# Reordering VectorE's work in the attention half of a two-layer hybrid encoder: rotary in two parts at other steps, low weight halves ahead of the attention step, two last output units interleaved

## The chip, the cores and the metric

The kernel runs on one core of one Trainium2 chip. A core has TensorE (PE, matrix multiply), VectorE (DVE), ScalarE (ACT), GpSimd (POOL) and SyncE (SP, which here only issues DMAs). The metric is the device time of one execution in microseconds, and lower is better. Times are medians of several executions.

## The reference, cut to what matters

```python
for l in range(2):
    u = rmsnorm(h, norm_g[l])
    p = u @ w_in[l]                      # 528 tokens x 1024, times 1024 x 9216
    hq, hf_f, hf_b, hi, hgt, aq, ak, av, agt = split(p)
    o_h = hgrn2_mixer(hq, hf_f, hf_b, hi, hgt, ...)      # 8 heads, gated linear recurrence
    o_a = diff_attention_mixer(aq, ak, av, agt, ...)     # 8 heads: rotary on q and k, two
                                         # softmaxes per head, p0 - lam * p1, times v, norm, gate
    h = h + concat(o_h, o_a) @ w_out[l]  # 2048 x 1024
return rmsnorm(h, final_norm_g)[:, 16:]
```

Rotary turns each pair of rows of q and k: `t1*c - t2*s, t2*c + t1*s`. Everything is float32.

## The kernel before, in words

Activations lie transposed: 128 rows of features on the partitions, 528 tokens (16 meta tokens and 512 real ones) along the free axis. All matrix work with weights is cut into **units**: one unit is 1024 x 128 weights, 8 **pieces** of 128 x 128. A layer has 89 units. To keep float32 accuracy with a rounded format, weights and activations are each split in a high and a low half, and a piece is three products (high-high, high-low, low-high), each in two matmuls of 264 tokens, so 6 matmuls; in layer 1, where only real tokens matter, units of q, gates and outputs take one matmul of 512 in place of two. Line 1256 is the matmul of every piece.

Each unit passes through a chain. SP loads `w_raw` (2 buffers) once `lo_cut` says that the raw buffer has been used; ACT copies it to `w_hi` (line 556, `cut_high`, 3 buffers), right after it evacuated the unit three places before; DVE subtracts to make `w_lo` (line 889, `cut_low`); PE runs the unit's 8 pieces into one of two PSUM buffers `proj`, and its first piece waits for `lo_cut` and for the buffer to have been evacuated. What follows a unit on DVE is `follow`: for `aq` and `ak` the rotary, which is a swap of neighbouring rows (line 983), two multiplications (lines 985 and 986) and an addition (line 991) into `gate_f`; for `outA` and `outB`, the units of the output projection, an addition onto `h` (line 943).

There is no planner at run time. Every engine executes a list written by the same loops: 16 heads per layer (0 to 7 HGRN2, 8 to 15 attention), and 13 **steps** per head. In each step an engine does its part of the head (`hgrn` or `attend`) and then its part of the units that feed the next head. PE spreads the next head's pieces over the steps by tables of shares (`HG_FEED`, `AT_FEED`, and `LAST_FEED` for head 15, where the fed units are `outB0` to `outB3`, with 7 pieces each, since the eighth needs head 15's own output). `units_after(c, s)` says which units PE has finished by the step before, so that ACT evacuates them at step s; `units_followed` says when DVE follows them, `units_cut` when DVE makes the low half of the unit three places on.

An attention head has 5 blocks of queries in layer 0 and 4 in layer 1 (128 queries, or the 16 meta tokens), each with two components, one per step. In a step PE makes the scores (4 matmuls, lines 1420 and 1422) in the one PSUM buffer `pair`; DVE takes the row maximum (line 1162, `neg_max`); ACT exponentiates (line 731, `decay`) and so frees `pair` for the next step's scores. In even steps from 2 on DVE combines the two softmaxes of the block before (lines 1181, 1183, 1191, `qk_dec`), PE transposes the result in the odd step after (lines 1449, 1450), ACT copies it out (lines 762, 765, `cols`), and PE multiplies it by v (lines 1435, 1437) one step later. DVE's order within a step before the change is: its part of the head, then `stack_low` if it is due, then `follow`, then the low half of a unit (`cut_after`).

Before head c's first scores, `gate_f` is split again: ACT makes the high halves in `q_stack` and `k_stack` (`stack_high`, line 774, after step 9 of the head before, after step 11 of head 7), DVE makes the low halves (`stack_low`, line 999, one step later), and SP copies them across partitions by DMA. In an attention head, the output of the head before is scaled, transposed and gated in steps 1 and 2 (lines 1101, 1117, `mixed_t`), rounded by ACT in step 3 (line 784, `mix_hi`) and its low half made by POOL (line 529, `mix_lo`). In head 15, the last piece of each `outB` unit (k = 6) needs this of head 14.

Of the kernel before, what the change touches and what calls it, by code (L numbers as in the profile page):

```python
# [38 lines left out]
HG_HEADS = 8  # L39
# [67 lines left out]
HG_FEED = (2, 3, 3, 3, 3, 3, 4, 4, 3, 3, 3, 4, 2)  # L107
AT_FEED = (3, 3, 3, 2, 2, 3, 2, 3, 2, 3, 2, 2, 2)

LAST_FEED = (2, 2, 1, 1, 3, 3, 3, 3, 2, 3, 2, 2, 1)  # L110

# [30 lines left out]
def pieces_per_unit(c):  # L144
    return EARLY_K if c == HEADS - 1 else KT


def pieces_by(c, s):

    if s < 0:  # L150
        return 0
    first, last = fed_units(c)
    pieces = (last - first) * pieces_per_unit(c)
    return round(share_fed(c, s) * pieces)


def units_after(c, s):

    first, _ = fed_units(c)
    n = pieces_per_unit(c)  # L160
    return range(first + pieces_by(c, s - 2) // n, first + pieces_by(c, s - 1) // n)


def unit_of(tile):
# [37 lines left out]
def units_followed(c, s):  # L202

    if c == HG_HEADS - 1:

        first = fed_units(c)[0]
        units = {TURN_KEYS: [first], TURN_KEYS + 1: [first + 1, first + 2]}.get(s, [])  # L210
    elif not HG_HEADS < c < HEADS - 1:
        units = [*units_after(c, s)]
    elif s % 2 == 1:
        units = [*units_after(c, s - 2), *units_after(c, s - 1)]
    else:
        units = []
    if s == 1 and c > 0:
        units = [*units_not_followed(c - 1), *units]
    return units


def units_not_followed(c):
# [6 lines left out]
def encoder_trunk(nc, x_t, w_units, norm_g, lb_logits, hg_gain, lambdas, at_gain, final_g,  # L229
# [12 lines left out]
    with ctx:  # L242
# [589 lines left out]
        def _(dve):  # L832
# [7 lines left out]
            def after(w):  # L840
                dve.wait_ge(dve_step, w)

            def prepare_lower_bounds():

                dve.wait_ge(consts_in, 16 * 8)
                w = step(dve.tensor_tensor(lb_work[:, 2, :], lb[:, 0, :], lb[:, 1, :], ALU.max))
                after(w)
                step(dve.tensor_tensor(lb_work[:, 0, :], lb[:, 0, :], lb_work[:, 2, :], ALU.subtract))
                dve.tensor_tensor(lb_work[:, 1, :], lb[:, 1, :], lb_work[:, 2, :], ALU.subtract)\
                    .then_inc(lb_max, 1)  # L850
                w = step(dve.tensor_tensor(lam_prod[:, :, :], lam_in[:, :, 0, :], lam_in[:, :, 1, :],
                                           ALU.mult))
                after(w)
                dve.tensor_reduce(lam_sum[:, :, :].rearrange("p a b -> p (a b)"), lam_prod[:, :, :],
                                  axis=X, op=ALU.add).then_inc(lb_max, 1)
                dve.wait_ge(lb_exp, 1)
                w = step(dve.tensor_tensor(lb_work[:, 2, :], lb_work[:, 0, :], lb_work[:, 1, :], ALU.add))
                after(w)
                w = step(dve.reciprocal(lb_work[:, 3, :], lb_work[:, 2, :]))
                after(w)  # L860
                step(dve.tensor_tensor(lb_work[:, 0, :], lb_work[:, 0, :], lb_work[:, 3, :], ALU.mult))
                w = step(dve.tensor_tensor(lb_work[:, 1, :], lb_work[:, 1, :], lb_work[:, 3, :], ALU.mult))
                after(w)
                w = step(dve.tensor_tensor(lb_work[:, 2, :], lb_work[:, 0, :], lb_work[:, 1, :], ALU.add))
                after(w)
                step(dve.tensor_tensor(lb[:, 0, :], lb_work[:, 0, :], lb_work[:, 0, :], ALU.subtract))
                w = step(dve.tensor_tensor(lb[:, 1, :], lb_work[:, 2, :], lb_work[:, 0, :], ALU.subtract))
                after(w)
                dve.tensor_scalar(one_minus_lb[:, :, :], lb[:, :, :], -1.0, 1.0, ALU.mult, ALU.add)\
                    .then_inc(bounds_ready, 1)  # L870
                dve.wait_ge(bounds_ready, 1)
                dve.wait_ge(lb_exp, 2)
                for l in range(DEPTH):
                    init = 0.8 - 0.6 * math.exp(-0.3 * l)
                    w = step(dve.tensor_tensor(lam[:, l:l + 1], lam_sum[:, l, 0:1], lam_sum[:, l, 1:2],
                                               ALU.subtract))
                    after(w)
                    step(dve.tensor_scalar(lam[:, l:l + 1], lam[:, l:l + 1], -1.0, -init, ALU.mult, ALU.add))

                    step(dve.tensor_scalar(g_at[:, l:l + 1], g_at[:, l:l + 1],  # L880
                                           math.sqrt(P) * (1.0 - init) * 0.5, None, ALU.mult))
                step(dve.tensor_scalar(g_hg[:, :], g_hg[:, :], math.sqrt(P), None, ALU.mult))
                w = step(dve.tensor_scalar(g_final[:, :], g_final[:, :], math.sqrt(D_MODEL), None, ALU.mult))
                after(w)
# [50 lines left out]
            def follow(l, i):  # L935
# [39 lines left out]
                elif what == "g":  # L975
                    dve.tensor_tensor(gates[:, c % 2, ts], a, b, ALU.mult).then_inc(stage_read, 1)
                elif what == "ag":
                    dve.scalar_tensor_tensor(gates[:, c % 2, ts], a, 1.0, b, ALU.add, ALU.mult)\
                        .then_inc(stage_read, 1)
                else:  # L980

                    d = 0 if what == "aq" else 1
                    w = step(dve.stream_shuffle(b, a, [r ^ 1 for r in range(32)]))  # L983
                    after(w)
                    step(dve.tensor_tensor(a, a, cos_sin[:, 0, ts], ALU.mult))
                    w = step(dve.tensor_tensor(b, b, cos_sin[:, 1, ts], ALU.mult))
                    after(w)
                    if c > HG_HEADS:

                        dve.wait_ge(stack_lo, 4 * (l * AT_HEADS + c - HG_HEADS))  # L990
                    dve.tensor_tensor(gate_f[:, d, ts], a, b, ALU.add).then_inc(stage_read, 1)

            def stack_low(a):

# [15 lines left out]
            def copy_meta_levels(g):  # L1010
                dve.wait_ge(level_done, g * LEVELS + META_LEVELS)
                w = step(dve.tensor_copy(score_meta[0:N_META, 0:N_META], meta[0:N_META, 0:N_META]))
                for lv in range(1, META_LEVELS):
# [4 lines left out]
                        w = step(ins)  # L1018
                    else:
                        ins.then_inc(meta_read, 1)  # L1020

            made = {}

            def total_pairs(lv):

# [175 lines left out]
            for l in range(DEPTH):  # L1201
# [5 lines left out]
                    cut_after(l, [i])  # L1207
                for c in range(HEADS):
                    for s in range(steps_of(c)):
                        (hgrn if c < HG_HEADS else attend)(l, c, s)  # L1210
                        if c == 0 and s == 1:
                            follow(l, len(HG_TILES) - 1)
                            cut_after(l, [len(HG_TILES) - 1])
                        if s == stack_step(c) + 1 and HG_HEADS <= c + 1 < HEADS:
                            stack_low(l * AT_HEADS + c + 1 - HG_HEADS)
                        for i in units_followed(c, s):
                            follow(l, i)
                        cut_after(l, units_cut(c, s))
                scale_output(l * HEADS + HEADS - 1)
                for i in units_not_followed(HEADS - 1):  # L1220
                    follow(l, i)
# [13 lines left out]
        def _(pe):  # L1235
# [40 lines left out]
                ins.then_inc(last_done if tile < EARLY_TILES - 1 else unit_done, 1)  # L1276

            def feed(l, c, s):
                first, _ = fed_units(c)
                in_unit = pieces_per_unit(c)  # L1280
                for q in range(pieces_by(c, s - 1), pieces_by(c, s)):
                    piece(l, first + q // in_unit, q % in_unit)

            def sum_squares(n):

# [276 lines left out]
```

## Time and profile before

| | |
|---|---|
| median of 3 runs | 1563.5 us (1562.32 to 1563.67) |
| the profiled execution | 1562.48 us |
| its span, first to last instruction | 1560.7 us |
| mean granted clock of TensorE | 0.994 |
| busy share of the span | PE 95%, weight loads 90%, DVE 65%, ACT 50%, POOL 6% |
| layer 0, attention half | from about 412 to 807 us |
| layer 1, attention half | from about 1184 to 1547 us |

The span is what the trace shows; 1.8 us of the execution lie around it. A busy share of PE is not its share of peak. Rows of a timeline show the start, the duration, the engine, the line, the operation, what it writes from what it reads, the shapes and the count; a bracket at the end is the idle time of the engine just before it, and what ended that. A `x2` row is two merged instructions.

### The profile page before, as it was taken

How to read it: one execution, taken by the hardware profiler on the slowest of the kernel's cores; microseconds unless marked ns; L12 is line 12 of the kernel's file. 1: busy time of each engine (PE TensorE's matmuls, PEld its weight loads, DVE VectorE, ACT ScalarE, POOL GpSimd, SP SyncE). 2: the span in 40 equal slices, each digit the busy share in tenths (PEclk: the TensorE clock that was granted, in tenths of full speed). 3: DMA queues.
4: the chain of work that ended last, by engine and by line, in shares of the span. 5: the costliest groups of instructions: out<-in, count | busy, mean ns of one | idle time of the engine just before them, and what ended most of it. 6: DMA issues, size and time to landing. Idle time of an engine off the chain costs nothing.

```text
span 1560.7 us, 27727 instructions
## 1 busy us (share of the span) xinstructions
PE 1489.2 (95%) x11148; PEld 1408.6 (90%) x11148; DVE 1006.7 (65%) x1720; ACT 773.4 (50%) x1689; POOL 90.4 (6%) x109
## 2 busy tenths in 40 slices
PE   5999999999999999999969999999998999999996
PEld 4999999999989999999969999999997789988874
DVE  6656666666644777777555666766676456766655
ACT  5445435544433566666435444454544346556542
POOL 0000000000000000000000000000000000000100
PEclk9999999999999999999989999999999999999998
DMA  4212112111213222222222212111112232222221
GB/s 158 82 55 68 55 56 67 55 55 55 62 62 96 83 68 69 69 69 69 64 72 68 68 55 68 56 67 58 65 59 64 70 107 69 68 81 70 82 71 65
DMA packets 34479, 109.38 MB, mean 70 GB/s; under 512 B 4912, under 2 KB 5040, under 8 KB 34352
## 3 DMA queue, kind: packets, MB, share of 16 engines
q1 hardware_dynamic: 34352, 107.61, 22.0%
q8 instruction: 89, 1.46, 0.4%
q14 instruction: 38, 0.31, 0.1%
HBM read 96.84 MB, written 2.10 MB: 63 GB/s over the span
## 4 chain that ended last, share of the span: by engine, by line
PE 83%; DVE 7%; issue 5%; ACT 2%; DMA 1%; SPq 1%; POOL 1%; DVEq 0%; ACTq 0%; POOLq 0%
PE proj L1256 56%; PE pair L1325 8%; PE meta L1435 3%; PE pair L1420 2%; PE pair L1422 2%; PE main L1449 2%; DVE w_lo L889 1%; DMA q_stack<-gate_f 1%; PE pair L1371 1%; PE main L1390 1%; PE main L1391 1%; DVE stage L983 1%; PE main L1305 1%; PE main L1332 1%; PE meta L1437 1%
## 5 line engine op out<-in xcount | busy, mean ns | idle before, releaser
L1256 PE MATMUL proj<-u_hi,w_hi 128*128 128x264 f32 (+1 forms) x2048 | 496.9, 314 | 19.4 <-DVE u_lo L925 13.9
L1256 PE MATMUL proj<-u_hi,w_lo 128*128 128x264 f32 (+1 forms) x2048 | 466.6, 299 | 0.0
L1256 PE MATMUL proj<-u_lo,w_hi 128*128 128x264 f32 (+1 forms) x2048 | 466.4, 299 | 0.0
L1256 PEld LDWEIGHTS proj<-u_hi,w_hi 128*128 128x128 f32 x2048 | 328.8, 191 | 33.6 <-issue 14.6
L1256 PEld LDWEIGHTS proj<-u_hi,w_lo 128*128 128x128 f32 x2048 | 327.0, 189 | 11.1
L1256 PEld LDWEIGHTS proj<-u_lo,w_hi 128*128 128x128 f32 x2048 | 327.4, 189 | 7.6
L889 DVE TENSOR_TENSOR w_lo<-w_raw,w_hi 128x1024 fp32r<-128x1024 f32 x178 | 216.8, 1219 | 58.5 <-ACT w_hi L556 58.5
L731 ACT ACTIVATE decay<-pair,neg_max 128x528 f32<-128x528 f32 (+1 forms) x144 | 100.7, 699 | 252.6 <-DVE neg_max L1162 252.5
L1162 DVE TENSOR_REDUCE neg_max<-pair 128x1 f32<-128x528 f32 (+1 forms) x144 | 101.4, 704 | 176.5 <-PE pair L1422 175.9
L556 ACT ACTIVATE w_hi<-w_raw 128x1024 fp32r<-128x1024 f32 x178 | 186.6, 1049 | 15.8 <-PE proj L1256 12.4
L677 ACT ACTIVATE qk_dec<-ops 128x528 f32<-128x528 f32 (+1 forms) x112 | 76.0, 679 | 116.9 <-DVE ops L1059 116.9
L1325 PE MATMUL pair<-ops,qk_dec 128*128 128x128 f32 x896 | 129.2, 288 | 0.0
L1325 PEld LDWEIGHTS pair<-ops,qk_dec 128*128 128x128 f32 x896 | 116.2, 191 | 2.5
L1256 PE MATMUL proj<-mix_hi,w_hi 128*128 128x264 f32 (+1 forms) x372 | 103.3, 332 | 7.8 <-issue 3.9
L1067 DVE TENSOR_TENSOR ops<-ops,totals 128x528 f32<-128x528 f32 (+1 forms) x96 | 67.2, 700 | 53.5 <-PE pair L1325 53.5
L1256 PE MATMUL proj<-mix_lo,w_hi 128*128 128x264 f32 (+1 forms) x372 | 99.3, 321 | 0.0
L1256 PE MATMUL proj<-mix_hi,w_lo 128*128 128x264 f32 (+1 forms) x372 | 99.2, 321 | 0.0
L1420 PE MATMUL pair<-k_stack,q_stack 128*128 128x264 f32 x288 | 78.5, 292 | 7.5 <-ACT decay L731 4.4
L529 POOL TENSOR_TENSOR mix_lo<-mixed_t,mix_hi 128x528 fp32r<-128x528 f32 (+1 forms) x32 | 42.5, 1327 | 734.7 <-ACT mix_hi L784 734.7
L1008 DVE COPY_PREDICATED score<-masks,pair 128x512 f32<-128x512 int32 x112 | 82.8, 740 | 0.0
L1435 PE MATMUL meta<-v_main,cols 128*128 128x128 f32 x576 | 76.7, 276 | 0.0
L1422 PE MATMUL pair<-k_low,q_stack 128*128 128x264 f32 x288 | 76.3, 286 | 0.0
(182 smaller groups left out, 2090.6 us busy)
## 6 DMA issues: line engine op xcount, KB each, us to landing
w_raw<-w_units SPq DMA_DIRECT2D x178, 512.0 KB, 3.5
k_stack<-k_stack SPq DMA_DIRECT2D x32, 132.0 KB, 2.3
q_stack<-gate_f SPq DMA_DIRECT2D x32, 132.0 KB, 2.4
h<-x_t SPq DMA_DIRECT2D x8, 264.0 KB, 4.7
out_t<-decay SPq DMA_DIRECT2D x4, 256.0 KB, 2.1
out_t<-ops SPq DMA_DIRECT2D x4, 256.0 KB, 2.1
cos_sin<-rope SPq DMA_DIRECT2D x1, 528.0 KB, 5.5
masks<-level_masks SPq DMA_DIRECT2D x1, 448.0 KB, 4.9
```

The source lines that it names most:

```text
L556: act.activation(w_hi[:, u % N_CUT, :, :], w_raw[:, u % N_RAW, :, :], ACT.Copy)\
L677: act.activation(dst, halves_of(c, KF, m, first, T - first), ACT.Copy).then_inc(k_copied, 1)
L731: act.activation(two(decay[0:rows, 2 * (i % 2) + comp, :]), pair[0:rows, :, both], ACT.Exp, bias=neg_max[0:rows, i % 2, comp:comp + 1], ac ...
L889: dve.tensor_tensor(w_lo[:, u % N_CUT, :, :], w_raw[:, u % N_RAW, :, :], w_hi[:, u % N_CUT, :, :].bitcast(f32), ALU.subtract).then_inc(lo_ ...
L1008: dve.copy_predicated(score[:, :, :], mask, src).then_inc(level_read, 1)
L1067: dve.tensor_tensor(queries, queries, facing_totals(m, QB), ALU.mult).then_inc(qk_ready, 1)
L1162: dve.tensor_reduce(neg_max[0:rows, i % 2, comp:comp + 1], pair[0:rows, :, both], axis=mybir.AxisListType.XY, op=ALU.max, negate=True)\
L1256: ins = pe.matmul(out, w, x[:, k, cols_n], start=(k == 0 and p == 0), stop=(k == last_k and p == 2))
L1325: ins = pe.matmul(pair[:, lv % 2, j * P:(j + 1) * P], k, q, start=True, stop=True)
L1420: pe.matmul(pair[0:rows, b, both], q_stack[:, comp, cs], k_stack[:, comp, keys], start=True, stop=False)
L1422: ins = pe.matmul(pair[0:rows, b, both], q_stack[:, comp, cs], k_low[:, comp, keys], start=False, stop=True)
L1435: pe.matmul(meta[:, 0:P], cols[:, kk, :], v_main[:, kk, :], start=(kk == 0), stop=False)
```

## The change

It changes only the order in which instructions are issued; none is added or removed. In every layer:

- The rotary of `ak` for heads 10 to 15 is split. The swap and the first multiplication stay at step 7 of the head before; the second multiplication and the addition (`finish_turn`) come in step 8, after DVE's part of that step.
- In head 7, `aq`'s rotary for head 8 goes from after step 9 to after step 8, and `ak`'s from after step 10 to after step 9.
- In head 8, `cut_after` comes before DVE's part of the step, not at its end.
- In head 15, `LAST_FEED` gives PE 3 pieces in each of steps 0 to 3, then 2 in each of steps 4 to 10, then 1, 1 (running totals 3, 6, 9, 12, 14, 16, ...; before they were 2, 4, 5, 6, 9, 12, 15, ...). The pieces of `outB0` and `outB1` are reordered: k = 0 to 5 of both, and then k = 6 of both. So both units end in step 4, and both are evacuated, and their successors `outB3` and `outB4` cut, in steps 5 and 6.
- The addition of an `outB` unit onto `h` comes before DVE's part of the step.

```diff
-LAST_FEED = (2, 2, 1, 1, 3, 3, 3, 3, 2, 3, 2, 2, 1)
+LAST_FEED = (3, 3, 3, 3, 2, 2, 2, 2, 2, 2, 2, 1, 1)
...
+def fed_pieces(c):
+    first, end = fed_units(c)
+    pieces = [(i, k) for i in range(first, end) for k in range(pieces_per_unit(c))]
+    if c == HEADS - 1:
+        late = EARLY_K - 1
+        two_units = [p for p in pieces if p[0] < first + 2]
+        pieces = [p for p in two_units if p[1] < late] + [p for p in two_units if p[1] == late] + \
+            pieces[len(two_units):]
+    return pieces
...
-    first, _ = fed_units(c)
-    n = pieces_per_unit(c)
-    return range(first + pieces_by(c, s - 2) // n, first + pieces_by(c, s - 1) // n)
+    earlier, now = pieces_by(c, s - 2), pieces_by(c, s - 1)
+    last = {i: at for at, (i, _) in enumerate(fed_pieces(c))}
+    return [i for i, at in last.items() if earlier <= at < now]
...
-        units = {TURN_KEYS: [first], TURN_KEYS + 1: [first + 1, first + 2]}.get(s, [])
+        units = {TURN_KEYS - 1: [first], TURN_KEYS: [first + 1, first + 2]}.get(s, [])
...
+def split_turn(c, i):
+    return HG_HEADS + 1 < c < HEADS and UNITS[i][0] == "ak"
+
+def turns_finished(c, s):
+    return [i for i in units_followed(c, s - 1) if split_turn(c + 1, i)] if HG_HEADS < c < HEADS - 1 and s else []
...
-                    w = step(dve.stream_shuffle(b, a, [r ^ 1 for r in range(32)]))
-                    after(w)
+                    made["swapped"] = step(dve.stream_shuffle(b, a, [r ^ 1 for r in range(32)]))
+                    after(made["swapped"])
                     step(dve.tensor_tensor(a, a, cos_sin[:, 0, ts], ALU.mult))
-                    w = step(dve.tensor_tensor(b, b, cos_sin[:, 1, ts], ALU.mult))
-                    after(w)
-                    if c > HG_HEADS:
-                        dve.wait_ge(stack_lo, 4 * (l * AT_HEADS + c - HG_HEADS))
-                    dve.tensor_tensor(gate_f[:, d, ts], a, b, ALU.add).then_inc(stage_read, 1)
+                    if not split_turn(c, i):
+                        finish_turn(l, i)
...
+                        ahead = [i for i in units_followed(c, s) if UNITS[i][0] == "outB"]
+                        for i in ahead:
+                            follow(l, i)
+                        if c == HG_HEADS:
+                            cut_after(l, units_cut(c, s))
                         (hgrn if c < HG_HEADS else attend)(l, c, s)
...
+                        for i in turns_finished(c, s):
+                            finish_turn(l, i)
                         for i in units_followed(c, s):
-                            follow(l, i)
-                        cut_after(l, units_cut(c, s))
+                            if i not in ahead:
+                                follow(l, i)
+                        if c != HG_HEADS:
+                            cut_after(l, units_cut(c, s))
...
-                for q in range(pieces_by(c, s - 1), pieces_by(c, s)):
-                    piece(l, first + q // in_unit, q % in_unit)
+                for i, k in fed_pieces(c)[pieces_by(c, s - 1):pieces_by(c, s)]:
+                    piece(l, i, k)
```

`finish_turn(l, i)` holds the three removed lines: it waits for the swap, multiplies `b` by the sines, waits for `stack_lo` and adds into `gate_f`.

## Rows read from the trace of the kernel before

**Rows 1.** The page: busy times, and the chain that ended last.

```profile
PE 1489.2 (95%) x11148; PEld 1408.6 (90%) x11148; DVE 1006.7 (65%) x1720; ACT 773.4 (50%) x1689; POOL 90.4 (6%) x109
...
PE 83%; DVE 7%; issue 5%; ACT 2%; DMA 1%; SPq 1%; POOL 1%; DVEq 0%; ACTq 0%; POOLq 0%
```

**Rows 2.** Busy time by engine in one attention head of layer 0 (length, PE, PEld, DVE, ...).

```profile
560.00:598.50 38.50, 38.10 (x320) 37.32 (x319) 27.66 (x49) 23.69 (x62) 2.76 (x3) 1.00 0.24 69
```

**Rows 3.** The waits, whole span: total us, times, longest us.

```profile
PE proj L1256 <- DVE w_lo L889: 5.5, 4, 1.7
PE main L1449 <- DVE qk_dec L1191: 4.9, 8, 0.7
PE pair L1420 <- ACT decay L731: 4.4, 10, 0.8
...
PE proj L1256 <- POOL mix_lo L529: 1.2, 3, 0.5
```

**Rows 4.** Timeline of PE, heads 9 to 14: layer 0, then layer 1.

```profile
569.32 0.40 PE L1256 MATMUL proj<-u_lo,w_hi 128*128 128x264 f32 x2
569.56 0.41 PE L1256 MATMUL proj<-u_hi,w_lo 128*128 128x264 f32 x2
570.37 0.29 PE L1420 MATMUL pair<-k_stack,q_stack 128*16 128x264 f32 x1 [0.40 <-ACT decay L731]
...
1296.09 0.63 PE L1449 MATMUL main<-ident,qk_dec 128*128 128x128 f32 x4 [0.69 <-DVE qk_dec L1191]
```

**Rows 5.** Timelines of DVE and ACT at the first of these places, layer 0.

```profile
566.26 0.70 DVE L986 TENSOR_TENSOR stage<-stage,cos_sin 128x528 f32<-128x528 f32 x1
...
567.62 1.22 DVE L889 TENSOR_TENSOR w_lo<-w_raw,w_hi 128x1024 fp32r<-128x1024 f32 x1
568.75 0.69 DVE L1162 TENSOR_REDUCE neg_max<-pair 16x1 f32<-16x528 f32 x1
...
573.13 0.63 ACT L774 ACTIVATE q_stack<-gate_f 64x528 fp32r<-64x528 f32 x1
```

**Rows 6.** Timelines of ACT, DVE and PE in head 8, layer 0.

```profile
415.79 1.07 ACT L556 ACTIVATE w_hi<-w_raw 128x1024 fp32r<-128x1024 f32 x1
...
420.40 0.71 DVE L1162 TENSOR_REDUCE neg_max<-pair 128x1 f32<-128x528 f32 x1 [6.36 <-PE pair L1422]
...
425.88 1.22 DVE L889 TENSOR_TENSOR w_lo<-w_raw,w_hi 128x1024 fp32r<-128x1024 f32 x1
...
427.15 0.51 PE L1256 MATMUL proj<-u_hi,w_hi 128*128 128x264 f32 x2 [1.12 <-DVE w_lo L889]
```

**Rows 7.** Timelines of DVE, ACT and PE in head 15: layer 0, then layer 1.

```profile
758.13 0.71 DVE L1162 TENSOR_REDUCE neg_max<-pair 128x1 f32<-128x528 f32 x1 [0.77 <-PE pair L1422]
...
758.87 0.70 ACT L731 ACTIVATE decay<-pair,neg_max 128x528 f32<-128x528 f32 x1 [2.27 <-DVE neg_max L1162]
...
760.67 0.28 PE L1420 MATMUL pair<-k_stack,q_stack 128*16 128x264 f32 x1
...
1505.61 0.71 DVE L1162 TENSOR_REDUCE neg_max<-pair 128x1 f32<-128x528 f32 x1 [0.64 <-PE pair L1422]
...
1507.52 0.25 ACT L765 ACTIVATE cols<-meta 16x128 f32<-16x128 f32 x1
...
1508.04 1.05 PE L1435 MATMUL meta<-v_main,cols 128*128 128x128 f32 x8
```

**Rows 8.** Entry to head 8: timelines of DVE, POOL and PE.

```profile
397.86 0.75 DVE L1117 SCALAR_TENSOR_TENSOR mixed_t<-main,g_hg,gates 128x512 f32<-128x512 f32 x1 [0.36 <-PE main L1332]
...
407.23 0.46 PE L1390 MATMUL main<-v_main,score 128*128 128x128 f32 x2 [1.21 <-DVE mixed_t L1129]
...
409.01 1.72 POOL L529 TENSOR_TENSOR mix_lo<-mixed_t,mix_hi 128x528 fp32r<-128x528 f32 x1 [35.41 <-ACT mix_hi L784]
...
412.54 0.39 PE L1420 MATMUL pair<-k_stack,q_stack 128*128 128x264 f32 x1 [0.71 <-DMA q_stack<-gate_f]
```

**Rows 9.** The tile k_low from 400 to 420 us: min/median/max ns, first and last start.

```profile
L999 DVE TENSOR_TENSOR k_low<-gate_f,k_stack x2: 705/1204/1703, 409.6 to 411.3; 64x528 fp32r<-64x528 f32 x2
```

More of the change, by code:

```diff
@@ L841, in after @@
                 dve.wait_ge(dve_step, w)
+            made = {}
             def prepare_lower_bounds():
@@ L980, in follow, with finish_turn @@
                 else:
-                    d = 0 if what == "aq" else 1
-                    w = step(dve.stream_shuffle(b, a, [r ^ 1 for r in range(32)]))
-                    after(w)
+                    made["swapped"] = step(dve.stream_shuffle(b, a, [r ^ 1 for r in range(32)]))
+                    after(made["swapped"])
                     step(dve.tensor_tensor(a, a, cos_sin[:, 0, ts], ALU.mult))
-                    w = step(dve.tensor_tensor(b, b, cos_sin[:, 1, ts], ALU.mult))
-                    after(w)
-                    if c > HG_HEADS:
-                        dve.wait_ge(stack_lo, 4 * (l * AT_HEADS + c - HG_HEADS))
-                    dve.tensor_tensor(gate_f[:, d, ts], a, b, ALU.add).then_inc(stage_read, 1)
+                    if not split_turn(c, i):
+                        finish_turn(l, i)
+            def finish_turn(l, i):
+                what, c, _, _ = UNITS[i]
+                use = (l * HEADS + c) * 3 + STAGE_USE[what]
+                ts = tokens(l, what)
+                a, b = stage[:, use % 2, 0, ts], stage[:, use % 2, 1, ts]
+                after(made["swapped"])
+                w = step(dve.tensor_tensor(b, b, cos_sin[:, 1, ts], ALU.mult))
+                after(w)
+                if c > HG_HEADS:
+                    dve.wait_ge(stack_lo, 4 * (l * AT_HEADS + c - HG_HEADS))
+                dve.tensor_tensor(gate_f[:, 0 if what == "aq" else 1, ts], a, b, ALU.add).then_inc(stage_read, 1)
             def stack_low(a):
@@ L1020, in copy_meta_levels @@
                         ins.then_inc(meta_read, 1)
-            made = {}
             def total_pairs(lv):
@@ L1278, in feed @@
             def feed(l, c, s):
-                first, _ = fed_units(c)
-                in_unit = pieces_per_unit(c)
-                for q in range(pieces_by(c, s - 1), pieces_by(c, s)):
-                    piece(l, first + q // in_unit, q % in_unit)
+                for i, k in fed_pieces(c)[pieces_by(c, s - 1):pieces_by(c, s)]:
+                    piece(l, i, k)
             def sum_squares(n):
```

## The prediction, made before the changed kernel ran

> **What bounds the kernel now.** I read the page first. PE is busy for 95% of the span and holds 83% of the chain that ended last, the other engines much less [rows 1]. So time can only come out of PE's idle time, and the question is where that lies. The busy time of one attention head shows how little there is: 38.10 of 38.50 us [rows 2]. Then I read the list of waits and kept the rows in which PE waits in the attention half: for a low weight half (5.5 us in 4 times), for the combined softmax `qk_dec` (4.9 us in 8), for an exponential (4.4 us in 10) and for POOL's `mix_lo` (1.2 us in 3) [rows 3]. The timelines say where these lie. The exponential is late once in each of heads 9 to 14 of layer 0, by 0.40 us; `qk_dec` is late once in each of heads 9 to 14 of layer 1, by 0.69 us [rows 4]; what is left of both rows, 4.4 - 6 x 0.40 = 2.0 us in 4 times and 4.9 - 6 x 0.69 = 0.8 us in 2, is in head 15, and so are two of POOL's three, 0.5 us each. The four waits for a low half are in head 8, two in each layer, and one of them stands in [rows 6].
>
> The column of idle time understates what a wait costs, because matmuls overlap. Pairs of matmuls start 569.56 - 569.32 = 0.24 us apart, so the scores that started at 570.37 could have started at 569.80: 0.56 us lost where the column says 0.40 [rows 4]. I add 0.16 us for each wait that goes, in both layers. One piece, three pairs, is 0.73 us of PE; layer 1's short ones are a little less.
>
> **The change, part by part.** No instruction is added or removed, so the work of every engine stays. Only waits can change.
>
> *Rotary in two parts, heads 9 to 14.* DVE executes in order. In step 7 it does `ak`'s four operations and a low half, and only then step 8: the row maximum, or in layer 1, which has no fifth block of queries, at once the combination. Moving the second multiplication and the addition behind them starts the low half at 566.26 in place of 567.62, so all that follows comes 1.36 us earlier [rows 5]. In layer 0 the row maximum moves from 568.75 to about 567.5, where its scores are ready, and the exponential with it, by 1.2 us against a lateness of 0.56. In layer 1 `qk_dec` comes 1.36 us earlier against 0.69 + 0.16 = 0.85. Both waits vanish. What is late instead is `gate_f`, now ready only after `qk_dec`, at about 568.6 + 0.7 + 1.4 = 570.7 us. ACT's `stack_high` takes it only after step 9's copies, at 573.13 us in this head [rows 5], so there are over 2 us of cover; if it were gone, the copies for the next head would come as much later as the cover lacks. The row maximum of step 9 stands behind the addition, and its scores end at about the same time, so that costs 0.1 us off PE's path. Gain: 6 x 0.56 + 6 x 0.85 = 8.4 us.
>
> *Low halves first in head 8.* Here head 8 feeds 96 pieces in place of 32, so weights run out faster. ACT had made the high half by 415.79 + 1.07 = 416.9 us, and DVE then sat idle for 6.36 us until its scores came at 420.40; but its list had the row maximum, the gate and a whole rotary ahead of the low half, which came at 425.88, and PE waited for it [rows 6]. Put first, it is done by 418.1 us, 9 us before PE asks. The second of each layer likewise comes right after the rotary before it, about 6 us ahead of need. What is queued behind a low half is now the row maximum, and behind that ACT's exponential and PE's next scores; I followed steps 1 to 7 and found the high half ready before the scores each time, at the tightest (steps 4 and 5) by about half a microsecond. PE's 6 or 9 pieces per step (4.4 or 6.6 us) hide a delay of that size too. Two other waits of PE in head 8, for `outA`'s addition onto `h`, are not touched, nor is POOL's third wait. Gain: 5.5 + 4 x 0.16 = 6.1 us.
>
> *Head 15.* PE waits here in steps 1 to 4, because with one or two pieces per step it is back at the scores before the exponential. With three pieces each step is 0.7 to 1.5 us longer, more than any of these waits, and the late k = 6 pieces are asked for in step 4 behind more work, so that `mix_lo` is there. Removed: 2.0 + 0.8 + 1.0 us idle in 8 waits, with 8 x 0.16 = 5.1 us. Part comes back. Both `outB0` and `outB1` now end in step 4, so step 6 has two low halves (1.14 us apart) where it had one, ahead of the row maximum of step 7; this had 0.77 us to spare in layer 0, and PE comes to it a piece (0.73 us) earlier. It is late by 1.14 + 0.73 - 0.77 = 1.10 us. The exponential then ended at 759.57 for scores at 760.67, a slack of 1.03 us with the signal's 0.07, of which another missing piece takes 0.73; PE waits 1.10 - 0.30 = 0.8 us. In layer 1 the products of step 8 need the copy that ended at 1507.77 and started at 1508.04; the row maximum had 0.64 us to spare: 1.14 + 0.7 - 0.64 = 1.2 late, and 1.2 + 0.7 - 0.27 = 1.6 us waited [rows 7]. Given back: 2.4 us. Bounds: nothing back, or all 5.1. The added `outB` ahead of the row maximum costs nothing: the second ends within 0.2 us of the time when the scores are ready, and the pieces behind cover that.
>
> *Entry to head 8.* DVE's 0.36 us of idle before the gate is filled by `aq`'s rotary, so PE's last products of head 7, which wait for DVE, start some 0.4 us earlier. But PE's first scores wait for a DMA of q's low half, and POOL's `mix_lo` ran from 409.01 to 410.73 [rows 8], beside a low half of k that took 1703 ns in place of 705 [rows 9]. `ak`'s rotary now ends earlier, ACT rounds earlier, and POOL's operation falls about 1.6 us sooner, on q's low halves, which the DMA waits for. I take 1.0 us more there less 0.5 us of earlier start, twice: 0.9 us lost. Bounds: 1.0 us gained in all if they miss each other, 2.0 lost.
>
> The Trainium skill (SBUF — State Buffer, "Who interferes with whom") says that a DVE instruction with two SBUF inputs and a GpSimd one that reads SBUF exclude each other, the first holding the shared port for its whole length. The 1703 ns agree with it in kind. By the rule the delay may be the whole POOL operation, 1.72 us, in place of 1.0; the sum would be 1.4 us poorer.
>
> **Sum.** 8.4 + 6.1 + 5.1 - 2.4 - 0.9 = 16.3 us. The profiled execution took 1562.5 us, so it would take 1546.2; it lies 1.0 us under the median of the runs shown, 1563.5, and for a median I predict 1547.2 us. At the bounds: the idle columns alone without head 15 (5.5 + 4.1 + 2.4 = 12.0) less 2.0 give 1553.5; all 19.6 plus 1.0 give 1542.9.
>
> **Rivals.** *Head 15 gives nothing* (chance 0.12): the late row maximum of step 7 eats all 5.1 us; 1563.5 - 13.6 = 1549.9. For it: DVE's queue there; against: only two steps per layer are touched. *Nothing comes back and the entry gains* (0.12): 1542.9. *Given back at the next fixed wait* (0.08): the 8.4 us of heads 9 to 14 reappear, for example at the copies for the next head; 1563.5 - 7.9 = 1555.6. Against: ACT's splitting follows PE's transposes, so the copies move with PE. *The change does not do what it says* (0.05): the gaps are moved and not closed, 1563. *Slower* (0.03), by one mechanism: in head 8 DVE, which executes in order, stands at a low half whose high half ACT has not made, and row maximum, exponential and scores stand behind it. There are 11 such cuts per layer. Without head 8's own gain the rest brings 10.2 us, so it decides from 0.46 us of PE wait per cut on; at 0.8 us the time is 1563.5 - 10.2 + 17.6 = 1570.9. Against: the 3.5 us between high half and row maximum [rows 6]. *The forecast* keeps 0.60, with 1545 to 1549 of its own.
>
> **How the numbers follow.** The range 1542 to 1554 holds the forecast, the first two rivals and the bounds, and leaves out 0.16. This kernel's measurement tells about 0.2%, 3 us, from no change. Faster: 0.60 + 0.12 + 0.12 + 0.08 = 0.92; within 0.2%: 0.05; slower: 0.03.
>
> **What would show it.** In the waits after: PE for `w_lo` gone; PE for `qk_dec` down from 8 times to none or two; PE for the exponential down from 10 times to one or two, now at step 8 of head 15 in layer 0; a new wait of 1 to 2 us before the products of step 8 in layer 1; a longer wait for the copy of q before head 8, with a low half of q at 1.7 us; head 9 to 14 periods shorter by 0.56 and 0.85 us. The prediction is wrong if waits for `outA`'s addition grow, if the copies for heads 10 to 15 become late, or if DVE idles before low halves in head 8 while its scores are ready.

## The result, and the profile after

| | before | after |
|---|---|---|
| median | 1563.29 us (4 runs, 1562.32 to 1563.67) | 1550.01 us (4 runs, 1549.52 to 1551.18) |
| profiled execution / its span | 1562.48 / 1560.7 us | 1549.82 / 1547.9 us |
| mean granted clock of TensorE | 0.994 | 0.989 |

The ratio is 0.9918, with a 95% interval of 0.9906 to 0.9931: 13.3 us or 0.8% faster. I forecast 1547.2 us. The page after, first line and chain, answers [rows 1]:

```profile
PE 1487.0 (96%) x11148; PEld 1410.0 (91%) x11148; DVE 1006.5 (65%) x1720; ACT 773.0 (50%) x1689; POOL 90.3 (6%) x109
...
PE 89%; DVE 4%; issue 3%; ACT 2%; DMA 1%; SPq 1%; POOL 0%; DVEq 0%; ACTq 0%; POOLq 0%
```

No engine does other work than before. DVE's share of the chain falls from 7% to 4%, as it should when PE waits less for it. The waits of the changed kernel, PE's rows and two of others, answer [rows 3] (total us, times, longest us):

```profile
DVE w_lo L914 <- ACT w_hi L579: 88.8, 48, 6.3
...
PEld pair L1459 <- DMA q_stack<-gate_f: 8.3, 8, 2.8
...
PE proj L1297 <- issue: 6.6, 5, 2.2
PE pair L1459 <- DMA q_stack<-gate_f: 4.5, 4, 2.3
PE proj L1297 <- DVE h L968: 2.2, 2, 1.1
PE meta L1474 <- ACT cols L788: 1.4, 2, 1.2
...
PE pair L1459 <- ACT decay L754: 0.5, 1, 0.5
PE proj L1297 <- POOL mix_lo L552: 0.2, 1, 0.2
```

PE has no row any more for `w_lo` or `qk_dec`, one wait for an exponential in place of ten and one for `mix_lo` in place of three. The row for `cols` is new and was forecast. Two rows are worse than before. The first is `proj <- issue`, for which the trace of before has this, with the row for `q_stack`:

```profile
PE proj L1256 <- issue: 3.9, 3, 1.5
PE pair L1420 <- DMA q_stack<-gate_f: 2.8, 6, 1.4
```

To find where the time went I compared the starts of PE's scores, step by step. Times are starts of the first scores of the step, in us; "the piece after head 15" is the one that waits for an addition onto `h` at the end of each layer.

| place | before | after | shift |
|---|---|---|---|
| layer 0, head 8, step 0 | 412.54 | 412.97 | +0.43 |
| step 1 | 419.71 | 421.64 | +1.93 |
| step 3 | 438.31 | 436.87 | -1.44 |
| step 9 | 480.27 | 478.63 | -1.64 |
| head 9, step 0 | 503.90 | 504.64 | +0.74 |
| head 15, step 0 | 735.18 | 732.92 | -2.26 |
| the piece after head 15 | 788.31 | 784.26 | -4.05 |
| layer 1, head 8, step 0 | 1183.97 | 1180.54 | -3.43 |
| step 7 | 1235.45 | 1228.71 | -6.74 |
| head 9, step 0 | 1268.72 | 1262.56 | -6.16 |
| head 15, step 0 | 1483.32 | 1471.92 | -11.40 |
| the piece after head 15 | 1531.96 | 1519.20 | -12.76 |

Three stretches gain as forecast: head 8's middle, heads 9 to 14, and head 15. Two lose what I had not in the sum: from step 9 of head 8 to head 9 (2.4 us in layer 0, 0.6 in layer 1), and the first step of head 8 in layer 0 (1.5 us).

**The first loss is a new wait.** DVE's timeline after, head 8 of layer 0, steps 9 and 10, and under it ACT's and PE's:

```profile
479.94 0.68 DVE L968 TENSOR_TENSOR h<-h,proj 128x528 f32<-128x528 f32 x1
485.12 1.23 DVE L914 TENSOR_TENSOR w_lo<-w_raw,w_hi 128x1024 fp32r<-128x1024 f32 x1 [4.50 <-ACT w_hi L579]
486.26 0.15 DVE L1213 RECIPROCAL row_inv<-row_sum 16x2 f32<-16x2 f32 x1
...
487.44 1.43 DVE L1033 TENSOR_TENSOR gate_f<-gate_f,q_stack 64x528 f32<-64x528 f32 x2
488.90 1.44 DVE L1033 TENSOR_TENSOR k_low<-gate_f,k_stack 64x528 fp32r<-64x528 f32 x2
490.37 0.70 DVE L968 TENSOR_TENSOR h<-h,proj 128x528 f32<-128x528 f32 x1
```

```profile
481.37 1.29 ACT L797 ACTIVATE q_stack<-gate_f 64x528 fp32r<-64x528 f32 x2
482.69 1.31 ACT L797 ACTIVATE k_stack<-gate_f 64x528 fp32r<-64x528 f32 x2
484.03 1.06 ACT L579 ACTIVATE w_hi<-w_raw 128x1024 fp32r<-128x1024 f32 x1
```

```profile
491.18 0.48 PE L1297 MATMUL proj<-mix_hi,w_hi 128*128 128x264 f32 x2 [2.21 <-issue]
```

The cut of step 10 stands first in DVE's step. ACT makes its high half only after the four copies of `stack_high`, at 484.03. DVE, idle since 480.6, holds for it for 4.50 us, and behind it in the queue stand the combination, four operations of `stack_low` and the addition onto `h` that empties a `proj` buffer. The addition ends at 491.07, and 0.11 us later PE starts the piece that needs the buffer, 2.21 us late. Before, that same addition ran at 487.43:

```profile
487.43 0.70 DVE L943 TENSOR_TENSOR h<-h,proj 128x528 f32<-128x528 f32 x1
```

The row names "issue" because the list does not see through PE's sequencer; DVE's rows do. In layer 1 the hold is 5.51 us, at 1246.47, and PE waits 0.54 us.

**The second loss is PE's clock.** Entry to head 8, POOL and DVE, PE, and then the tile `gate_f` (min/median/max ns), answering [rows 8, 9]:

```profile
407.18 1.54 POOL L552 TENSOR_TENSOR mix_lo<-mixed_t,mix_hi 128x528 fp32r<-128x528 f32 x1 [33.76 <-ACT mix_hi L807]
407.48 2.54 DVE L1033 TENSOR_TENSOR gate_f<-gate_f,q_stack 64x528 f32<-64x528 f32 x2
410.05 1.44 DVE L1033 TENSOR_TENSOR k_low<-gate_f,k_stack 64x528 fp32r<-64x528 f32 x2
```

```profile
406.57 0.46 PE L1429 MATMUL main<-v_main,score 128*128 128x128 f32 x2 [0.73 <-DVE mixed_t L1161]
...
412.97 0.40 PE L1459 MATMUL pair<-k_stack,q_stack 128*128 128x264 f32 x1 [1.80 <-DMA q_stack<-gate_f]
```

```profile
L1033 DVE TENSOR_TENSOR gate_f<-gate_f,q_stack x2: 706/1254/1803, 407.5 to 409.3; 64x528 f32<-64x528 f32 x2
```

PE waits 1.80 us for the copy of q where it waited 0.71. That much I had forecast. Behind this wait come windows that I had not. Busy time by engine after, and then before (length, PE, PEld, DVE, ACT, POOL, PE's granted clock, DMA share, GB/s):

```profile
412.00:414.00 2.00, 1.03 (x8) 1.03 (x9) 0.23 (x1) 1.44 (x3) 1.44 (x2) 1.00 0.97 277
414.00:416.00 2.00, 2.00 (x13) 2.00 (x13) 0.47 (x1) 1.49 (x4) 0.00 (x0) 0.62 0.10 37
416.00:418.00 2.00, 2.00 (x11) 2.00 (x10) 0.72 (x1) 1.25 (x2) 0.00 (x0) 0.52 0.00 0
418.00:420.00 2.00, 2.00 (x19) 2.00 (x18) 0.51 (x1) 0.00 (x0) 0.00 (x0) 1.00 0.27 61
```

```profile
414.00:416.00 2.00, 2.00 (x19) 2.00 (x18) 0.04 (x1) 1.99 (x6) 0.41 (x1) 1.00 0.03 8
416.00:418.00 2.00, 2.00 (x19) 2.00 (x18) 0.00 (x0) 0.86 (x1) 0.00 (x0) 1.00 0.00 0
```

PE is busy all of 414 to 418 in both, but 13 and 11 rows start in place of 19 and 19: the clock is at the lower of its two levels (1.2 GHz in place of 2.4) for most of 3 us. From the first scores of head 8 to the next is 421.64 - 412.97 = 8.67 us, before 419.71 - 412.54 = 7.17. So the fall costs 1.5 us, more than the 1.1 us by which the wait that precedes it is longer. Most of the lower mean clock after (0.989 for 0.994) is not this fall but a stretch at the start, 16 to 32 us (0.66 and 0.70 over its two halves, 1.00 before). It cost little: PE's transposes in head 7 start at 399.68 us, before at 399.84.

### The profile page after: what moved, and what is told of

It reads as the page before. It is cut to its first block, busy times and chain, and to the rows that moved or that the text cites. A ratio compares the mean times of both kernels' runs of the same rounds, so it can differ in the third digit from the quotient of the medians.

```text
span 1547.9 us, 27727 instructions
## 1 busy us (share of the span) xinstructions
PE 1487.0 (96%) x11148; PEld 1410.0 (91%) x11148; DVE 1006.5 (65%) x1720; ACT 773.0 (50%) x1689; POOL 90.3 (6%) x109
## 4 chain that ended last, share of the span: by engine, by line
PE 89%; DVE 4%; issue 3%; ACT 2%; DMA 1%; SPq 1%; POOL 0%; DVEq 0%; ACTq 0%; POOLq 0%
PE proj L1297 60%; PE pair L1364 8%; PE meta L1474 4%; PE pair L1459 2%; PE pair L1461 2%; PE main L1488 2%; DMA q_stack<-gate_f 1%; PE meta L1476 1%; PE main L1429 1%; PE main L1430 1%; PE pair L1410 1%; PE main L1344 1%; PE main L1371 1%; DVE w_lo L914 1%; DVE mixed_t L934 1%
## 5 line engine op out<-in xcount | busy, mean ns | idle before, releaser
L1297 PEld LDWEIGHTS proj<-u_hi,w_hi 128*128 128x128 f32 x2048 | 329.4, 191 | 27.3 <-issue 14.6
L1297 PEld LDWEIGHTS proj<-mix_hi,w_hi 128*128 128x128 f32 x372 | 61.6, 189 | 17.4 <-issue 9.7
```

What stands on the lines that cost most here:

```text
L1297: ins = pe.matmul(out, w, x[:, k, cols_n], start=(k == 0 and p == 0), stop=(k == last_k and p == 2))
```

## The experiments

Each is the changed kernel with one edit, or with parts of the change undone. The three kernels of the first group and the first kernel of the second shared their runs of the kernel before (median 1562.82 us); the last four shared others (1562.86 us).

### One part of the change at a time

**The rotary alone**: the changed kernel with `aq` and `ak` of head 7 at their old steps, `cut_after` last everywhere, and head 15 as before.

```diff
-LAST_FEED = (3, 3, 3, 3, 2, 2, 2, 2, 2, 2, 2, 1, 1)
+LAST_FEED = (2, 2, 1, 1, 3, 3, 3, 3, 2, 3, 2, 2, 1)
...
-    if c == HEADS - 1:
+    if False:
...
-        units = {TURN_KEYS - 1: [first], TURN_KEYS: [first + 1, first + 2]}.get(s, [])
+        units = {TURN_KEYS: [first], TURN_KEYS + 1: [first + 1, first + 2]}.get(s, [])
...
-                        ahead = [i for i in units_followed(c, s) if UNITS[i][0] == "outB"]
+                        ahead = []
...
-                        if c == HG_HEADS:
-                            cut_after(l, units_cut(c, s))
...
-                        if c != HG_HEADS:
-                            cut_after(l, units_cut(c, s))
+                        cut_after(l, units_cut(c, s))
```

> The kernel before with one part of the change: the rotary of ak for heads 10 to 15 in two parts. My theory, which adds up the waits that each part removes: the shifts of the traces give 3.0 us for heads 9 to 14 of layer 0 and 5.2 us for those of layer 1, so 8.2 us: 1555.1 us against 1563.3. The rival, that PE's waits come back at the next fixed point when the other parts are missing: 3 us or less, 1560 us or more.

Measured: 1554.57 us, against 1562.82 for the kernel before; ratio 0.9948 (0.9933 to 0.9963), 8.3 us. In the trace head 9 of layer 0 starts at -0.31 and head 15 at -3.42 us, in layer 1 at -2.93 and -8.26: 3.1 + 5.3 us out of heads 9 to 14. Its list of waits has what is left in head 15:

```profile
PE pair L1456 <- ACT decay L754: 2.0, 4, 0.8
...
PE main L1485 <- DVE qk_dec L1223: 0.7, 2, 0.5
```

These are the 2.0 us in 4 times and 0.8 in 2 (0.7 here) that I had worked out from [rows 3, 4] as head 15's share.

**The low halves first alone**: `split_turn` returns False, head 7 and head 15 as before, `cut_after` first in head 8.

```diff
-    return HG_HEADS + 1 < c < HEADS and UNITS[i][0] == "ak"
+    return False
...
-        units = {TURN_KEYS - 1: [first], TURN_KEYS: [first + 1, first + 2]}.get(s, [])
+        units = {TURN_KEYS: [first], TURN_KEYS + 1: [first + 1, first + 2]}.get(s, [])
```

> The kernel before with one part: low halves before DVE's part of the step in head 8. Theory: the four waits for w_lo go (the scores of step 3 come 3.4 us earlier in layer 0 and 3.3 us in layer 1) and a new wait of PE appears in step 10 (2.2 us in layer 0, 0.5 in layer 1, with some 0.1 to 0.2 us more each), because the low half put first waits for ACT's high half and stack_low and outA's addition stand behind it: 6.7 - 3.0 = 3.7 us, 1559.6 us. PE waits 0.7 us for the DMA of q before head 8 in layer 0 as before, and the granted clock stays 1.0 there. Rival: the new wait in step 10 comes from the other parts of the change (the earlier PE), and this part alone gives all 6.1 us: 1557.2 us.

Measured: 1559.89 us, for 1559.6 by the theory; ratio 0.9979 (0.9970 to 0.9989), 2.9 us, where the waits that go are worth more than 6. The new wait is here in full, though nothing else of the change is:

```profile
489.63 0.48 PE L1297 MATMUL proj<-mix_hi,w_hi 128*128 128x264 f32 x2 [2.17 <-issue]
```

So it comes from the place of the cut and from nothing else. In this execution the clock fell behind it as well:

```profile
488.00:492.00 4.00, 2.37 (x12) 2.40 (x13) 3.22 (x5) 0.00 (x0) 0.00 (x0) 0.77 0.64 132
492.00:496.00 4.00, 4.00 (x29) 3.82 (x29) 0.01 (x1) 1.23 (x3) 0.00 (x0) 0.81 0.29 113
```

Layer 0 went from -3.18 us at step 9 of head 8 to +0.72 at head 9: 3.9 us lost in place of 2.4, so again 1.5 us for a fall. At the entry to head 8 the wait is the old 0.7 us and the clock 1.00.

**Head 15 alone**: the new `LAST_FEED`, the two interleaved units and the addition of `outB` first; the rest undone.

```diff
-    return HG_HEADS + 1 < c < HEADS and UNITS[i][0] == "ak"
+    return False
...
-        units = {TURN_KEYS - 1: [first], TURN_KEYS: [first + 1, first + 2]}.get(s, [])
+        units = {TURN_KEYS: [first], TURN_KEYS + 1: [first + 1, first + 2]}.get(s, [])
...
-                        if c == HG_HEADS:
-                            cut_after(l, units_cut(c, s))
...
-                        if c != HG_HEADS:
-                            cut_after(l, units_cut(c, s))
+                        cut_after(l, units_cut(c, s))
```

> The kernel before with one part: head 15 (LAST_FEED, the order of outB0 and outB1, outB's addition first). Theory: 1.8 us in layer 0 and 1.3 us in layer 1, so 3.1 us: 1560.2 us, with PE waiting 0.5 us for the exponential of step 7 in layer 0 and 1.2 us for the copy before step 8's products in layer 1. Rival: the waits of head 15 depend on where head 14 leaves DVE (its ak rotary in step 7), and this part alone gives under 1.5 us.

Measured: 1559.65 us; ratio 0.9980 (0.9971 to 0.9990), 3.2 us. In its trace head 15 gives 1.8 us in layer 0 and 1.4 us in layer 1, by the same marks as in the table above, and PE waits 0.5 us for the exponential and 1.2 us for the copy: what the changed kernel has too. So head 15's gain does not hang on head 14's new rotary.

The three parts alone sum to 8.3 + 2.9 + 3.2 = 14.4 us; the whole change brings 13.3, and the only part not among the three is head 7's. The intervals are 1.5 to 2.3 us to either side, so these medians alone do not show that head 7's part costs anything; the traces below do.

### One loss undone at a time

**The cut of step 10 goes last again**, those of steps 0 to 8 stay first (head 8 only):

```diff
+FIRST_S = 9
...
-                        if c == HG_HEADS:
+                        if c == HG_HEADS and s < FIRST_S:
...
-                        if c != HG_HEADS:
+                        if not (c == HG_HEADS and s < FIRST_S):
```

> The changed kernel, but with low halves first in head 8 only up to step 8; from step 9 on they come last, as in the kernel before. Theory: the new wait before outA6 in step 10 (2.21 us in layer 0, 0.54 in layer 1) goes and nothing else does: 3.0 us less than the changed kernel, 1547.0 us against 1550.0. Rival: that wait is for outA's own addition whatever stands before it, since PE now comes earlier: at most 1 us less, 1549 us or more.

Measured: 1547.88 us, against 1562.82; ratio 0.9904 (0.9890 to 0.9919). DVE's timeline, in the same stretch as above:

```profile
480.55 1.21 DVE L915 TENSOR_TENSOR w_lo<-w_raw,w_hi 128x1024 fp32r<-128x1024 f32 x1
...
484.32 1.44 DVE L1034 TENSOR_TENSOR k_low<-gate_f,k_stack 64x528 fp32r<-64x528 f32 x2
485.79 0.70 DVE L969 TENSOR_TENSOR h<-h,proj 128x528 f32<-128x528 f32 x1
486.41 1.22 DVE L915 TENSOR_TENSOR w_lo<-w_raw,w_hi 128x1024 fp32r<-128x1024 f32 x1
```

The addition onto `h` comes at 485.79 in place of 490.37, and the cut after it finds its high half ready. PE's row for `issue` is back at 3.9 us in 3 times. Head 8's step 9 and head 9's start now both stand at -1.6 us, where the changed kernel went from -1.64 to +0.74. The span is 2.7 us shorter. The entry to head 8 is as in the changed kernel, fall of the clock included (0.79 over 412 to 420).

**Head 7's rotary at its old steps**, all else of the change kept:

```diff
-        units = {TURN_KEYS - 1: [first], TURN_KEYS: [first + 1, first + 2]}.get(s, [])
+        units = {TURN_KEYS: [first], TURN_KEYS + 1: [first + 1, first + 2]}.get(s, [])
```

> The changed kernel with head 7's rotary back at its old steps. Theory: the earlier rotary is a loss, because it puts POOL's mix_lo on the low halves of q. Without it PE's waits for the copy of q fall from 1.8 and 2.3 us to 0.7 and 1.4, while PE's wait before head 7's last products rises by 0.5 in each layer; net 1.0 us, and the stretch of half clock in step 0 of head 8 in layer 0 (1.5 us) goes too, if it comes from the long wait: 1547.5 us against 1550.0. Rival: the earlier rotary is worth its 0.5 us a layer and the half clock is chance: 1550 to 1551 us.

Measured: 1548.27 us, against 1562.86; ratio 0.9907 (0.9892 to 0.9921), 14.6 us, which is the 14.4 of the three parts alone. The wait for q and the tile `gate_f`:

```profile
412.02 0.39 PE L1459 MATMUL pair<-k_stack,q_stack 128*128 128x264 f32 x1 [0.70 <-DMA q_stack<-gate_f]
```

```profile
L1033 DVE TENSOR_TENSOR gate_f<-gate_f,q_stack x2: 692/698/705, 407.6 to 408.3; 64x528 f32<-64x528 f32 x2
```

Both low halves of q are fast, and the clock is 1.00 from 412 to 420. The part of the change in head 7 costs, then: 1.3 us if each is taken against its own runs of the kernel before (14.6 and 13.3), 2.5 us between the two spans, of which 1.5 are the fall of the clock and 0.4 lie ahead of it all, in the start of head 7's transposes (399.32 for 399.68). By the ratios the two kernels are not told apart, since their intervals overlap; that the earlier rotary brings the long wait and the slow low half is shown by the rows.

**POOL's rounding later**: head 7's rotary stays early, and in head 7 `mix_hi` and `mix_lo` (the output of head 6) are made a step later, so that POOL runs after `stack_low`.

```diff
-    return HG_STEPS - 2 if c < HG_HEADS else 3
+    return HG_STEPS - 1 if c == HG_HEADS - 1 else HG_STEPS - 2 if c < HG_HEADS else 3
```

> The changed kernel, but in head 7 ACT rounds the mixed output of head 6 after step 12 in place of step 11, so that POOL's mix_lo starts after VectorE has made the low halves of q and k. Theory, that the two engines shut each other out: q's low halves take 0.7 us each, none 1.8; the DMA of q is issued 1.1 us earlier in both layers, PE's waits for it fall from 1.8 and 2.3 us to 0.7 and 1.3, and the half clock in step 0 goes: 2.2 + 1.5 = 3.7 us, 1546.3 us; 1547.8 if the half clock stays. Rival: the slow low half comes from the DMAs of k that run beside it: nothing changes, 1550 us.

Measured: 1547.30 us; ratio 0.9900 (0.9884 to 0.9917). The tile `gate_f`, POOL and PE:

```profile
L1033 DVE TENSOR_TENSOR gate_f<-gate_f,q_stack x2: 694/700/705, 407.5 to 408.2; 64x528 f32<-64x528 f32 x2
...
L1033 DVE TENSOR_TENSOR k_low<-gate_f,k_stack x2: 702/705/708, 408.9 to 409.7; 64x528 fp32r<-64x528 f32 x2
```

```profile
412.77 1.33 POOL L552 TENSOR_TENSOR mix_lo<-mixed_t,mix_hi 128x528 fp32r<-128x528 f32 x1 [39.33 <-ACT mix_hi L807]
```

```profile
411.91 0.39 PE L1459 MATMUL pair<-k_stack,q_stack 128*128 128x264 f32 x1 [0.74 <-DMA q_stack<-gate_f]
```

With POOL away all four low halves take 0.7 us, the first scores start 1.06 us earlier than in the changed kernel, and the clock is 1.00 from 412 to 420. SP issues the two DMAs of k at 406.29 us in this kernel and in the changed one, so the rival, that they slow the low half, is out. In this execution the clock fell behind the other wait instead, the one of step 10: 0.79 over 488 to 496, and 3.9 us lost there (-4.09 to -0.19) where the changed kernel lost 2.4.

**One low half less before the row maximum in head 15**: the cuts of `outB3` and `outB4`, both in step 6, go to steps 6 and 7.

```diff
+    if c == HEADS - 1 and s in (6, 7):
+        return [*units_after(c, 5)][s - 6:s - 5]
```

> The changed kernel, but in head 15 the low half of outB4 comes at the end of step 7, not as the second one of step 6. Theory: the row maximum of step 7 is no longer late, PE's 0.5 us for the exponential in layer 0 and 1.2 us before step 8's products in layer 1 go, with 0.1 to 0.2 us more each: 1.9 us, 1548.1 us. Rival: it is late because ACT makes two high halves (2 us) ahead of the exponential of step 6: the waits stay, 1550 us.

Measured: 1548.85 us; ratio 0.9915 (0.9900 to 0.9929). By the median this is not to be told from the changed kernel. The waits tell more: the row for the exponential is gone, and that for `cols` is down from 1.4 to 0.5 us in 2 times; and by the marks of the table head 15 gives 2.6 us in layer 0 and 2.3 in layer 1 in place of 1.8 and 1.4, so 1.8 us more, for 1.9 in the theory. In this execution the clock fell at both waits (0.79 in 412 to 420, 0.79 in 488 to 496), so its span of 1546.7 holds a fall more than that of the changed kernel.

**All three together**: the last cut of head 8 last, the later rounding, the cuts spread in head 15.

> The changed kernel with the three edits at once: low halves first in head 8 only up to step 8, head 6's rounding after step 12 of head 7, and outB4's low half in step 7. Theory: the gains add up, 2.1 to 3.0 + 3.7 + 1.9 = 7.7 to 8.6 us under the changed kernel, 1541.4 to 1542.3 us. Rival: what one frees another takes back, since all lie on the same two engines: 1544 us or more.

Measured: 1540.93 us (4 runs, 1540.78 to 1542.18), against 1562.86; ratio 0.9862 (0.9847 to 0.9876), 21.9 us or 1.4% faster than before and 9.1 us under the changed kernel. The theory had 1541.4 to 1542.3. Its waits, and its windows behind the places of the two losses:

```profile
PE proj L1300 <- issue: 3.9, 3, 1.5
PE pair L1462 <- DMA q_stack<-gate_f: 2.2, 4, 1.3
```

```profile
412.00:416.00 4.00, 4.00 (x33) 4.00 (x34) 0.71 (x1) 3.97 (x9) 2.76 (x3) 1.00 0.28 109
416.00:420.00 4.00, 4.00 (x36) 3.98 (x34) 1.47 (x2) 0.81 (x1) 0.00 (x0) 1.00 0.23 52
488.00:492.00 4.00, 4.00 (x35) 3.82 (x34) 0.37 (x1) 1.23 (x3) 0.00 (x0) 1.00 0.96 269
```

The wait for q is down to 0.67 us and over at 411.90, and the one of step 10 is gone: PE is busy for the whole of each window, at the full level.

## Why the prediction was right, and which terms were off

The time lies in the range, 2.8 us above the forecast, and outside the 1545 to 1549 us that I had kept for the forecast itself. It is within 0.1 us of what I gave for the rival that head 15 gives nothing, 1549.9; that is chance, since head 15 gave 3.2 us. The three gains are those I named, by the steps I named. Two terms are missing from the sum: one that I did not follow, and one that no row of before could show. In the trace, by the table of starts:

| term | forecast | measured | how |
|---|---|---|---|
| heads 9 to 14 | 8.4 | 8.2 | 0.74 + 2.26; 11.40 - 6.16 |
| head 8, waits for low halves | 6.1 | 6.9 | 1.93 + 1.64; 6.74 - 3.43 |
| head 15 | 5.1 - 2.4 = 2.7 | 3.2 | 4.05 - 2.26; 12.76 - 11.40 |
| entry to head 8 | -0.9 | -1.1 | 0.43; 4.05 - 3.43 (with all that lies before it) |
| head 8, step 10 | 0 | -3.0 | 1.64 + 0.74; 6.74 - 6.16 |
| the clock | 0 | -1.5 | 8.67 - 7.17 |

They sum to 12.7 us by the rounded rows and 12.8 by the table, the change of the span; the two profiled executions differ by 12.7 us, the medians by 13.3. Neither "entry" is the entry alone: each holds the stretch since the last marked place, where two executions can differ by up to 0.9 us that have nothing to do with the change: the kernel with head 15 alone starts head 8 of layer 0 at +0.87 us, with nothing changed up to there.

- *Heads 9 to 14*: right. DVE's rows for head 10 of layer 0 stand as forecast, with the low half at 566.53, the row maximum at 567.70, and the multiplication and the addition behind the combination at 569.51 and 570.25; the addition ends 2.0 us before ACT's `stack_high` at 572.92. The scores that waited to 570.37 start at 570.08. In layer 0 about 0.5 us per head stays, not 0.56: 0.57 goes at step 9 and up to 0.1 comes back before the next head; I did not follow that.
- *Head 8's low halves*: right, and 0.8 us richer than forecast. In the table of starts each of the four waits that went gives 0.26 to 0.30 us more than its idle time, where I had added 0.16, and 0.2 us more goes at step 8 of layer 0; I did not follow either. One reading was loose: DVE's 6.36 us of idle began at 414.04, ahead of ACT's high half at 416.9, so 3.5 us of it lie behind that, the figure that I used further down. PE waits no more for `w_lo`; only its weight loads show it, 2.7 us in 2 times.
- *Head 15*: the eight waits of steps 1 to 4 are gone, and the wait before step 8's products in layer 1 is there, at 1.19 us for a forecast of 1.6. In layer 0 0.49 us (757.33, before the scores of step 8) and 0.22 (763.51) came back for 0.8. The 0.07 us that I took for the signal stands in no row of mine; from the low half to PE's piece it is 0.05 us in [rows 6] (427.10 to 427.15), too little to matter. That the late row maximum behind two low halves makes these waits is borne out by the run that spreads the cuts: 0.5 us and 1.4 us of waiting become 0 and 0.5.
- *Entry to head 8*: right in mechanism, and in size by the rows of the waits. PE's wait for q grew by 1.80 - 0.71 = 1.09 us in layer 0 and 2.34 - 1.44 = 0.90 in layer 1, and its wait before head 7's last products shrank by 1.21 - 0.73 = 0.48 and 1.27 - 0.74 = 0.53: 1.0 us lost for a forecast of 0.9. POOL's `mix_lo` ran at 407.18, on the low halves of q, of which one took 1803 ns; with POOL moved behind them none did. The delay was 1803 - 706 = 1.1 us. POOL's operation began at 407.18 and ended at 408.72; DVE's began at 407.48, and what POOL still had to do was 1.24 us. The Trainium skill (SBUF — State Buffer, "Who interferes with whom") says that such a pair exclude each other, and that the one that comes second waits until the first is done. The trace agrees: the second lost 1.10 of those 1.24 us. So what an overlap cost here is the rest of the first one, not all of it. POOL's operation took 1.54 us itself, against 1.33 us when alone; it began under the low weight half that DVE ended at 407.56, and I did not follow that.
- *Step 10 of head 8*: **the step that failed**. I wrote that "I followed steps 1 to 7 and found the high half ready before the scores each time". Steps 8 to 12 I did not follow. There ACT's queue has `stack_high`, 2.6 us long, ahead of the high half, and DVE's has `stack_low` and an addition for PE behind the low half. What I gave as the rival on the slower side, DVE held at a low half, is the mechanism. DVE was in fact held at six cuts of head 8 in layer 0 and seven in layer 1 (0.41 us in all before), by up to 6.27 us at 1239.13, and in steps 1 to 7 this cost PE nothing, as I had found. PE was late behind one hold per layer, and who waited at its end was not the row maximum but the addition onto `h`. I had also written that PE's two waits for `outA`'s addition in head 8 "are not touched". Those two are the same: 1.54 us at 460.99 and 1.53 at 1231.21 before, 1.54 at 459.56 and 1.53 at 1224.47 after, each right behind an addition onto `h`. They stand in the row for `issue`, and the two new ones, 2.21 and 0.54 us, stand beside them there; the row for `h` (2.2 us in 2) is of the pieces after head 15. The kernel with this one cut last does not lose these 3.0 us. My own sign for this, "if DVE idles before low halves in head 8 while its scores are ready", was near it but named the wrong waiter: step 10 of head 8 has no scores.
- *The clock*: not in the sum at all. The trace of before gave no cause: over the attention half of layer 0 its longest wait of PE is 1.69 us, and the granted clock is 1.00 behind it.

A rival theory held that the new wait comes from the earlier pace of the other parts. The run with the low halves first alone excludes it. What stays open is which executions have a fall of the clock. Each kernel has one trace; it is likely, but not shown, that its other executions differ in this. So between kernels whose waits are both near 2 us a difference of 1 to 2 us may be the clock's.

## What to carry to other kernels

Moving an instruction to the front of its engine's step makes everything of that step wait for its input: check the move in each step of the loop, above all in the ones with an irregular list, and not in those where the gain is. When the parts of a change seem to bring less together than alone, look in the traces at the part that was not tried alone; here undoing it, or moving what it collides with, was worth 1.3 and 2.3 us by medians whose intervals overlap, and the waits in the traces settled it. Price a stall of the bound engine of about 2 us by more than its length, if the trace shows that the clock can fall behind it.

## What the runs showed of the hardware

Windows of the changed kernel behind two longer waits, 2.21 us at 491.18 and 2.34 us at 1180.54:

```profile
492.00:496.00 4.00, 4.00 (x36) 3.82 (x35) 0.82 (x2) 1.23 (x3) 0.00 (x0) 1.00 0.42 133
...
1180.00:1184.00 4.00, 3.46 (x17) 2.94 (x18) 0.71 (x1) 2.04 (x6) 0.45 (x1) 1.00 0.38 132
1184.00:1188.00 4.00, 4.00 (x24) 3.47 (x23) 1.23 (x1) 0.80 (x1) 0.00 (x0) 1.00 0.25 60
```

PE's clock fell to its lower level behind single waits of 1.80 to 2.21 us in the attention half of layer 0, six times in five traces, and each fall cost 1.5 us, by the starts of the scores around it. It is not decided by the wait's length alone. In the changed kernel it fell behind 1.80 us and not behind 2.21. In step 10 of head 8 it fell behind 2.17 us in the kernel with the low halves first alone, and with head 7's rotary back it stayed at 1.00 behind 2.17 us:

```profile
488.84 0.48 PE L1297 MATMUL proj<-mix_hi,w_hi 128*128 128x264 f32 x2 [2.17 <-issue]
```

It fell in the run with the later rounding behind the second (0.74 us at the first); with the cuts spread behind both; and in layer 1, behind 2.34 us at 1180.54, the clock was 1.00 from 1180 to 1188. Behind waits of 0.7 us at the entry to head 8 it never fell in these traces, nor behind the other waits of 1.0 to 1.7 us inside the attention halves (1.69 us at 436.01 before). The Trainium skill (TensorE: Matmul & The Clock Gate, "What's actually happening") says that the level follows how busy the engine has lately been, and that the point at which it changes varies from run to run. The traces agree with the first: in the attention halves it fell only behind waits of 1.8 us and more, and in every trace it fell at the change of layers, with waits of 4.9 and 6.6 us; that equal waits of 2.17 us ended both ways fits the second, which one trace per kernel cannot show.
